# Gated delta rule on one core: a Pool-written first turned inverse, and a last level that forms the turned inverses itself

## What is computed

```python
def _chunk_gated_delta(q, k, v, g, beta, state0):      # C = chunk
    a_mat = jnp.where(strict, jnp.einsum('bhnid,bhnjd->bhnij', kb, k) * decay, 0.0)
    t_mat = lax.linalg.triangular_solve(eye + a_mat, eye, lower=True, unit_diagonal=True)
    u = einsum(t_mat, vb);  w = einsum(t_mat, kb * exp(gc))
    def step(s, inp):
        v_new = u_i - einsum(w_i, s)
        o_i = einsum(qd_i, s) + einsum(qk_i, v_new)
        s = s * gl_i + einsum(kd_i, v_new)
        return s, o_i
```

## Time and profile before

| | before |
|---|---|
| median of 3 runs | 2777.19 us |
| run that was profiled | 2777.59 us |
| its span on the core | 2775.8 us |
| PE busy | 2504.4 us (90%) |
| DVE, ACT, Pool busy | 1235.8, 995.8, 163.1 us |
| chain that ended last | PE 74%, DVE 13%, ACT 8%, issue 3%, Pool 1% |
| transposes (L132) | 1190, 179.2 us busy |
| mean granted clock of TensorE | 0.955 of 2.4 GHz |

### The profile page before, as it was taken

One profiled execution on the slowest core, in us unless ns is written; L12 is line 12 of the kernel. 1 busy time (PEld: TensorE's weight loads), 2 busy tenths in 40 slices (PEclk: granted clock), 3 DMA queues, 4 the chain that ended last, 5 costly groups with the idle time before them and its releaser, 6 DMA issues.

```text
span 2775.8 us, 29478 instructions
## 1 busy us (share of the span) xinstructions
PE 2504.4 (90%) x11930; PEld 1963.3 (71%) x11930; DVE 1235.8 (45%) x1976; ACT 995.8 (36%) x1753; POOL 163.1 (6%) x210
## 2 busy tenths in 40 slices
PE   6998798799999898689999998989988899899999
PEld 4776576467878675578878887866555688688887
DVE  3343534336536434455665565333344433443342
ACT  3244243333222222444444444334433322342231
POOL 0000000000000000101111112100111000000000
PEclk9999899899999896899999999999999999999999
DMA  3211122015445321000000000011001123233232
GB/s 148 77 61 61 49 88 84 23 53 189 166 145 196 104 79 35 31 16 16 24 23 24 24 16 9 31 55 37 15 14 53 46 94 126 69 99 93 97 99 84
DMA packets 57447, 190.92 MB, mean 69 GB/s; under 512 B 6369, under 2 KB 11233, under 8 KB 56929
## 3 DMA queue, kind: packets, MB, share of 16 engines
q1 hardware_dynamic: 57312, 189.04, 20.5%
HBM read 184.82 MB, written 4.19 MB: 68 GB/s over the span
## 4 chain that ended last, share of the span: by engine, by line
PE 74%; DVE 13%; ACT 8%; issue 3%; POOL 1%; DMA 0%; SPq 0%; DVEq 0%; ACTq 0%
PE ps L129 70%; ACT sb L141 5%; DVE sb L162 5%; PE ps L132 4%; DVE sb L154 3%; DVE r L154 2%; ACT L139 2%; DVE sb L159 2%; DVE sb L171 1%; ACT r L141 1%; ACT sb L142 1%; POOL sb L154 1%; DVE sb L145 0%; DMA sb<-in_w_aq 0%; DVE sb L174 0%
## 5 line engine op out<-in xcount | busy, mean ns | idle before, releaser
L129 PE MATMUL ps<-r 128*128 128x512 f32 (+1 forms) x6552 | 1561.6, 397 | 64.7 <-DVE r L154 54.9
L129 PEld LDWEIGHTS ps<-r 128*128 128x128 f32 x6552 | 1227.0, 191 | 372.6 <-issue 68.8
L129 PE MATMUL ps<-sb 128*128 128x128 f32 (+6 forms) x4188 | 870.5, 356 | 111.5 <-ACT sb L141 80.9
L129 PEld LDWEIGHTS ps<-sb 128*128 128x128 f32 (+1 forms) x4188 | 614.2, 201 | 309.3 <-issue 149.7
L154 DVE TENSOR_TENSOR r<-sb,r 128x1024 fp32r<-128x1024 f32 (+3 forms) x429 | 434.9, 1021 | 638.6 <-ACT r L141 637.9
L141 ACT ACTIVATE r<-sb 128x1024 fp32r<-128x1024 f32 (+3 forms) x429 | 371.5, 887 | 541.4 <-PE ps L129 318.2
L141 ACT ACTIVATE sb<-ps 128x512 f32<-128x512 f32 (+3 forms) x620 | 270.3, 456 | 672.9 <-PE ps L129 528.3
L162 DVE SCALAR_TENSOR_TENSOR sb<-sb 128x512 f32<-128x512 f32 (+5 forms) x240 | 225.5, 950 | 116.6 <-ACT sb L141 115.6
L154 DVE TENSOR_TENSOR sb<-ps,sb 128x512 f32<-128x512 f32 x252 | 147.4, 596 | 282.6 <-PE ps L129 277.0
L132 PE MATMUL ps<-sb 128*128 128x128 f32 x1190 | 179.2, 287 | 91.9 <-DVE sb L154 22.1
L132 PEld LDWEIGHTS ps<-sb 128*128 128x128 f32 x1190 | 139.2, 146 | 127.0 <-DVE sb L159 42.0
(11 more groups left out here) (23 smaller groups left out, 164.1 us busy)
## 6 DMA issues: line engine op xcount, KB each, us to landing
sb<-in_w_mlp SPq DMA_DIRECT2D x64, 512.0 KB, 3.5
sb<-in_w_mod SPq DMA_DIRECT2D x48, 512.0 KB, 4.4
sb<-in_w_qkv SPq DMA_DIRECT2D x24, 512.0 KB, 3.3
sb<-in_w_g SPq DMA_DIRECT2D x22, 512.0 KB, 3.3
sb<-in_w_u SPq DMA_DIRECT2D x22, 512.0 KB, 3.3
sb<-in_w_out SPq DMA_DIRECT2D x16, 512.0 KB, 3.4
sb<-in_w_down SPq DMA_DIRECT2D x16, 512.0 KB, 3.6
sb<-in_w_gate SPq DMA_DIRECT2D x16, 512.0 KB, 3.3
```

The source lines that it names most:

```text
L129: return QUIET if self.e is None else self.e.matmul(o, l, r, start=start, stop=stop)
```

## The change

Level 0: the transposes of TF and TB, and ACT's copies of them, go. Pool instead writes V_ right after its identities: it multiplies N_ by a constant pattern "pair" (one neighbour for each row) and subtracts the product from the identity, two instructions a batch, each behind a wait for Pool's own result before.

Level 6: at level 5 ACT now copies both turned inverses whole into U, where it copied half of the columns into V_. b_y2 of level 6 has the operands the other way round (Y_ stationary, U moving), so that its result is the correction of the turned inverses, and DVE subtracts it from U. The transposes and copies of level 6 go. The chain's c_x waits for DVE's b_t of level 6 in place of ACT's copies, and the next head's b_x waits for b_y1 of level 6 in place of the last transposes.

The number of yields stays as it was in all parts. The constants grow by 128 columns in one DMA.

```diff
-C2 = {"negF": 128, "negB": 128, "lev": 896}
+C2 = {"negF": 128, "negB": 128, "lev": 896, "pair": 128}
@@ batch_pe
-                    fence(e, [("b_y", h, i, lv), ("b_uc", h, i, 1, lv - 1)] + free[b])
+                    fence(e, [("b_y", h, i, lv), ("b_uc", h, i, 1, lv - 1) if lv > 1 else ("b_v0", h, i, 1)] + free[b])
                     for j in range(nb):
-                        m = e.matmul(P(b * 512 + j * 128, 128), S(V_ + j * 128, 128), S(Y_ + j * 128, 128), True, True)
+                        if lv < 6:
+                            m = e.matmul(P(b * 512 + j * 128, 128), S(V_ + j * 128, 128), S(Y_ + j * 128, 128), True, True)
+                        else:
+                            m = e.matmul(P(b * 512 + j * 128, 128), S(Y_ + j * 128, 128), mixed_cols(UB + j * 128, 64, 128, UF - UB),
+                                         True, True)
...
-                for d in range(2):
+                for d in range(2) if 0 < lv < 6 else ():
                     b = take()
                     fence(e, [("b_t", h, i, lv)] + free[b])
@@ batch_dve
-                    e.wait_ge(*at("b_tr", h - 1, i, 1, 6))
+                    e.wait_ge(*at("b_y1", h - 1, i, 6))
...
-                t = mixed_cols(TF, s, W_, TB - TF)
+                t = mixed_cols(TF, s, W_, TB - TF) if lv < 6 else mixed_cols(UB, s, W_, UF - UB)
@@ batch_act
-                for d in range(2):
+                for d in range(2) if 0 < lv < 6 else ():
...
-                    if lv < 6:
-                        v = e.act(pat(V_ + f_, s, nb),
-                                  P(o + f_, (128, nb), 64) if s == 64 else P(o + f_, (128, nb), (2 * s, 64 // s), s), ACT.Copy)
+                    if lv < 5:
+                        v = e.act(S(V_ + f_, (128, nb), (2 * s, 64 // s), s), P(o + f_, (128, nb), (2 * s, 64 // s), s), ACT.Copy)
@@ batch_pool
+            e.wait_ge(*at("b_na", h, i))
+            e.tt(four(S, V_, nb), four(S, N_, nb), S(O2["pair"], (0, nb), (1, 128)), MU).then_inc(*up("b_v0", h, i, 0))
+            e.wait_ge(*at("b_v0", h, i, 0))
+            e.tt(four(S, V_, nb), S(CO["ident"], (0, nb), (1, 128)), four(S, V_, nb), SU).then_inc(*up("b_v0", h, i, 1))
             yield
@@ chain_pe
-                fence(e, [("b_uc", h, u, d, 6), ("c_r", h, d, n) if n else ("rows", 3 * h + 2, 1)] + free[k])
+                fence(e, [("b_t", h, u, 6), ("c_r", h, d, n) if n else ("rows", 3 * h + 2, 1)] + free[k])
```

More of the change, by code:

```diff
@@ L60 @@
          **{x: "gates_by_dve" for x in ("g_bgt", "g_c", "g_n", "g_ng", "g_td", "g_y", "g_z")},
-         **{x: "gates_by_act" for x in ("g_l", "g_e", "g_ne", "g_sig")}, "eps5": "eps", "eps6": "eps", "eps_q": "eps", "l_add": "pool_add", "l_uqn": "l_uq",
+         **{x: "gates_by_act" for x in ("g_l", "g_e", "g_ne", "g_sig")}, "eps5": "eps", "eps6": "eps", "eps_q": "eps", "l_add": "pool_add", "l_uqn": "l_uq", "b_v0": "b_na",
          "uq": "m0", "uk": "m1", "uv": "m2", "c1_in": "table_in", "c2_in": "table_in", "c3_in": "table_in",
@@ L1651, in four @@
             return f(o, (128, nb), 128)
-        def pat(o, s, nb):
-            return S(o, (128, nb), 64) if s == 64 else S(o, (128, nb), (2 * s, 64 // s), s)
         def mixed_cols(o, s, n, step):
@@ L1662, in batch_pe @@
             N_, V_, TF, TB, Y_ = NTY[i]
+            UF, UB = UU[h % 2][i]
             q, kk = HEADS[h % 3][:2]
@@ L2803, in _tables @@
     cM[64:], sM[64:] = cM[:64], sM[:64]
-    c2 = [np.where(b >= a, 0.0, NEG), np.where(b <= a, 0.0, NEG), *lev]
+    pair = np.where(b // 2 % 2 == 1, (a % 2 == 0) & (b == a + 1), (a % 2 == 1) & (b == a - 1))
+    c2 = [np.where(b >= a, 0.0, NEG), np.where(b <= a, 0.0, NEG), *lev, pair]
     c3 = [cM, sM]
```

## The result

| | before | changed |
|---|---|---|
| median, timed together | 2775.53 us (4 runs) | 2791.27 us (4 runs) |
| ratio to before | | 1.0057 [1.0045, 1.007] |
| profiled run, span | 2777.59, 2775.8 us | 2791.74, 2790.0 us |
| records of transposes (L132) | 1190 | 998 |
| mean granted clock | 0.955 | 0.944 |

A forecast was written before the change was run, and what follows sets the result against it. TensorE was taken to bound the step, though not everywhere in it. Level 6 -13.5, level 0 -10.9, Pool's wait +21.9 and clock +11.1 gave +8.6 us on 2777.59: 2786.2 us, 8-in-10 range 2769 to 2797.

The forecast's parts named there:

- level 6: End of a head: without wait and transposes TensorE goes on 1.65 us earlier a step; 13.5 us less in all.
- level 0: Transposes gone from TensorE's unbroken stretch: 1.28 us less a step in six heads, 10.9 us less in all.
- c_kd later: Pool's queue: four new instructions ahead of c_kd of n = 1 delay it by 3.3 us.
- Pool's wait: TensorE's c_u waits for the delayed c_kd: 3.05 us more in steps 2 to 7, 21.9 us in all.
- clock: Longer pause ahead of c_u halves TensorE's clock: 2.1 us more in steps 3 to 7, 11.1 us in all.
- The four sums: Whole-kernel totals: level 6 -13.5, level 0 -10.9, Pool's wait +21.9, clock +11.1, together +8.6 us.
- the terms of steps 1 and 8: Step 1: 0.6 us less at level 0; step 8: 2.6 less there, 3.6 more for Pool's wait.
- The first: At TensorE's pause ahead of c_u the clock holds, or falls in few steps: -2.5 us, 2775 us; chance 0.24.
- The second: TensorE's idleness ahead of c_u isn't Pool's, or other work absorbs the delay: -24.4, 2753 us; chance 0.11.
- The third: Pool's new instructions cost 4.9 to 5.3 us a step, like its adds beside DVE: about 2799 us; chance 0.12.
- The fourth: The edit fails its aim, as when level 6's turned product makes TensorE wait anew: near 2783 us; chance 0.03.

The follow-up runs named there:

- e6: Kernel before, with 6 and 7 matmuls that nobody reads filling TensorE's two pauses; 2771.09 us, ratio 0.9984.
- e9: Kernel before with the change's level-6 part alone and both pauses filled by 6 and 7 unread matmuls; 2758.09 us, ratio 0.9946.
- e5: e1 with both pauses filled by 6 and 7 matmuls that nobody reads; 2747.51 us, ratio 0.99.
- e10: e5 without the 7 matmuls in the second pause, so only the first is filled; 2748.65 us, ratio 0.9912.
- e3: Changed kernel with 16 unread matmuls ahead of the first c_u of n = 1, filling Pool's pause; 2772.21 us, ratio 0.9989.
- e1: Changed kernel with Pool's four new instructions a head issued one yield later, behind c_kd; 2767.39 us, ratio 0.9969.
- e4: Kernel before plus Pool's four new instructions a head, written to unused SBUF, transposes and copies kept; 2817.22 us, ratio 1.0151.
- e8: e1 with Pool's identities also behind c_kd, 10 unread matmuls ahead of q's sum of squares, 7 in the second pause; 2755.45 us, ratio 0.993.
- e7: Kernel before with 7 more unread matmuls ahead of the level-6 transposes in each head, where no pause is; 2800.24 us, ratio 1.009.
- e2: Changed kernel with level 0 as before, leaving the level-6 part alone, pauses unfilled; 2773.58 us, ratio 0.9993.

## Why the prediction was right, and where it was not

The lengths over 1500 us in the table run from the start of step 1 (Pool's first mask) to the end of the span, in the profiled runs; they leave out the part ahead of the change, whose length varies by up to 3 us from run to run.

| term | forecast | measured |
|---|---|---|
| level 6, a step | -1.65 | 78.66 to 76.83 (e6, e9): -1.83 |
| level 6, all | -13.5 | 1612.58 to 1599.05 (e6, e9): -13.5 |
| level 0, a step | -1.28 | 76.83 to 75.55 (e9, e5): -1.28 |
| level 0, all | -10.9 | 1599.05 to 1588.83 (e9, e5): -10.2 |
| c_kd later | 3.3 | 3.53 |
| Pool's wait, a step | +3.05 | 75.36 to 78.34 (e10, e3): +2.98 |
| Pool's wait, all | +21.9 | 1588.87 to 1612.66 (e10, e3): +23.8, with one fall of the clock in it |
| clock, steps 3 to 6, each | +2.1 | 78.34 to 81.46 and up to 81.85 (e3, changed): +3.1 to +3.5 |
| clock, all | +11.1 | 1612.66 to 1632.42 (e3, changed): +19.8; less 5.5: +14.3 |

In the last row 5.5 us go off because the forecast counts over the kernel before, which had falls of its own: filling takes it from 1618.11 to 1612.58 us (e6). The four sums make +14.4 us, and the two profiled runs differ by 14.3 from step 1 on.

**Level 6 and level 0** were right in mechanism and size, at an unbroken clock. The kernels e6, e9 and e5 differ by these parts alone, Pool's instructions being in e5 but out of the way. By the ratios, which are less sharp, the two parts are some 10.5 and 12.8 us.

**Pool** was right, and "issue" was read rightly: e1 shows it by taking the queue away, e4 by adding it alone, e8 by moving the wait and the idleness together. c_kd came 0.2 us later than reckoned, because the first product took 1.50 us beside the end of DVE's convolution and not the 1.27 of the forecast. In the chain of waits of the changed kernel it is the first piece here, and the gap of 0.07 us behind it is Pool's wait for itself, for which I had taken 0.05:

```profile
1328.45 1.50 POOL sb L154
1329.95 0.07 issue
1330.02 1.77 POOL sb L154 x2
```

The broadcast read beside a free DVE takes 1.07 us. The 1.77 us of the third line hold the difference of batch 0 and the add of batch 1, so the add did get back to some 0.7 us, as the contention rule of the Trainium skill (GPSIMD Engine Reference, section Specifications) had it.

**The clock** was right in its sign and too small, and this is the term that failed. I had taken it from one pause of like length in step 1, as one loss a step, of 2.1 us. In place of that, the clock fell at two pauses in each of the steps 3 to 7, the second one old and only 1.76 us long, and the two together cost 3.1 to 3.5 us in steps 3 to 6. Both losses are on the path. One short fall costs 1.6 us (e7), so the 2.1 were rather high for one, which hid a part of the one that was missing. The profiled run tells the same by step: 16.5 us more in steps 3 to 7, where the forecast's terms make 5 x 2.22 = 11.1.

In step 8 the clock was low for 20 us in place of 14 (in the changed kernel 3.4 us from 1724.0 and 17.1 from 1730.8), which the forecast had left out. So 2.2 us more stand behind that step's start, where the forecast had some 0.8 less. Step 1 went the other way, 5.4 us less where I had 2.25: one of its two late falls is gone. That the terms of steps 1 and 8 are off by about 3 us each, with opposite signs, left no trace in the sum. That is luck.

**The rivals.** The first (the clock holds, 2775 us) did not come; it is near what e3 made on purpose, 2772 us. The second (no wait for Pool) is refuted by e1, e4 and e8. The third (2799 us) named the wrong cause: the time did end above the forecast, but Pool's instructions cost 3.5 us a step and not 4.9. The fourth is refuted by e9: a step gains all of the forecast's 1.65 us, so the turned product brings no wait.

What the forecast also assumed, without a word, is that a gain on PE is kept once it is on the path. e1 and e2 show otherwise. In e1 two falls of 1.5 us ate what had been taken out of a step, until the pauses were filled. e2 alone has some 13 us of gain by e9, and could not be told from no change.

**What stays open** is why the falls come. The pauses of 1.42 and 1.76 us are the same in the kernel before, which has no fall in five steps, in e1, which has two in each, and in e7, which has one or two with more work. Either can come without the other (e3, e7), and yet filling the first alone kept the second away in five steps (e10). All this fits a dependence on the moment at which a pause comes, which the length of the step carries on from one to the next. But no run here varied that moment by itself, so it is argued and not shown.

## What to carry to other kernels

An engine that is busy for 6% of the time can still have a queue that the bound engine waits for: before adding to it, find the next instruction behind the new ones and who waits for that. Work without a near reader belongs behind it; here one yield was worth 24 us. Where TensorE pauses in every pass of a loop, price a change at an unbroken clock and with falls, and test it with the pauses filled by matmuls that nobody reads: here that gave each part its price at a clock of 1.00, and the fastest kernel.

## What was not expected of the hardware

Filling pauses with matmuls that compute nothing made kernels faster: 19 us in the changed one (2791.27 to 2772.21), 20 us in e1 (2767.39 to 2747.51, on two chips; by the ratios 19), 4.5 us in the kernel before. A fall of the granted clock from 1.00 to 0.50 at a pause of 1.4 to 1.8 us costs 1.5 to 1.6 us of a step (80.04 to 81.68 in e7) and may not come at all in the same place of a kernel that is 0.1 us a step different (78.43 in the kernel before, 78.53 in e1). And 1.6 us of added work a step (78.45 to 80.04) cost 3.1 us a head (e7).
